# A hybrid retention / HGRN2 / MoE layer: split projections, and the values and gates of all heads ahead of the recurrence

## What is computed

```python
def hg_dir(p, z, lb):
    q = jax.nn.silu(to_heads(p[4], HG_HEADS))
    lbh = lb.reshape(1, HG_HEADS, 1, HG_DK)
    f = lbh + (1.0 - lbh) * jax.nn.sigmoid(to_heads(z, HG_HEADS))
    return q, 1.0 - f, to_heads(p[7], HG_HEADS), jnp.log(f)
...
"""S_t = diag(a_t) S_{t-1} + k_t v_t^T ; o_t = S_t^T q_t, chunkwise."""   # forward and backward, summed
...
b = from_heads(rms_norm(o_hg, hg_norm_w_l)) * jax.nn.silu(p[8])
```

## Time and profile before

| | |
|---|---|
| median of 3 runs | 2821.18 us (2820.17 to 2823.1) |
| profiled execution, its own time | 2818.32 us |
| its span, first to last instruction | 2816.7 us |
| mean granted TensorE clock | 0.978 |
| busy: TensorE, VectorE, ScalarE, GpSimd | 94%, 74%, 51%, 19% |
| `hgrn2` in it | 48.6 to 556.7 us |

### The profile page before, as it was taken

The page is one execution under the profiler, slowest core; times in us unless marked ns, Lnnn a source line. Parts: engine busy times, 40 slices in busy tenths (PEclk is TensorE's granted clock), DMA queues, the critical chain, the costliest instruction groups (busy, mean ns, idle before and its releaser), DMA issues. The chain is left out here.

```text
span 2816.7 us, 43469 instructions
## 1 busy us (share of the span) xinstructions
PE 2651.4 (94%) x15273; PEld 2208.2 (78%) x15274; DVE 2079.2 (74%) x2433; ACT 1426.4 (51%) x1442; POOL 543.3 (19%) x437
## 2 busy tenths in 40 slices
PE   7899999899798899999999999999999999999994
PEld 3668577577687779777887978899989897888783
DVE  4566676673666796999879787866686778967884
ACT  4433535331634574777647565544454546645653
POOL 0524434200013211222121111111121112111110
PEclk9999999999899899999999999999999999999997
DMA  7101100180353796999969787866586769967864
GB/s 260 31 23 31 30 24 16 49 289 1 118 137 124 289 381 218 367 354 351 320 221 363 259 294 262 283 203 205 192 293 207 256 235 329 326 207 272 300 227 134
DMA packets 266663, 596.96 MB, mean 212 GB/s; under 512 B 21373, under 2 KB 47141, under 8 KB 265473
## 3 DMA queue, kind: packets, MB, share of 16 engines
q1 hardware_dynamic: 246208, 552.82, 54.9%
q0 software_dynamic: 20384, 43.19, 6.9%
HBM read 578.01 MB, written 42.25 MB: 220 GB/s over the span
## 5 line engine op out<-in xcount | busy, mean ns | idle before, releaser
L2100 ACT ACTIVATE whi<-e_slot 128x2048 fp32r<-128x2048 f32 x296 | 560.9, 1912 | 437.2 <-PE e_acc L2026 370.8
L2162 DVE TENSOR_TENSOR e_slot_r<-e_slot,whi 128x2048 fp32r<-128x2048 f32 x296 | 674.9, 2287 | 101.1 <-ACT whi L2100 101.1
L2023 PE MATMUL e_acc<-e_xhi,whi 128*128 128x256 f32 x1664 | 399.4, 282 | 3.2 <-ACT e_xhi L2104 3.2
L2100 ACT ACTIVATE whi<-slot 128x2048 fp32r<-128x2048 f32 x148 | 283.3, 1914 | 192.1 <-PE e_acc L1998 192.1
L2162 DVE TENSOR_TENSOR slot_r<-slot,whi 128x2048 fp32r<-128x2048 f32 x151 | 344.7, 2285 | 19.7 <-ACT whi L2100 16.7
L1996 PE MATMUL e_acc<-whi,e_ahi 128*128 128x512 f32 x800 | 319.4, 399 | 0.0
L2023 PEld LDWEIGHTS e_acc<-e_xhi,whi 128*128 128x128 f32 x1664 | 313.1, 188 | 6.3 <-ACT e_xhi L2104 6.3
L1940 POOL DMA_INDIRECT sum<-yo,e_idx_now x50 | 122.3, 2446 | 1012.3 <-issue 539.4
L1998 PE MATMUL e_acc<-whi,e_alo 128*128 128x512 f32 x800 | 313.4, 392 | 0.0
L1997 PE MATMUL e_acc<-e_slot_r,e_ahi 128*128 128x512 f32 x800 | 311.6, 389 | 0.0
L1996 PE MATMUL e_acc<-whi,e_xhi 128*128 128x512 f32 x768 | 303.3, 395 | 0.8 <-DVE e_slot_r L2162 0.5
(11 more groups left out here) (338 smaller groups left out, 4794.8 us busy)
## 6 DMA issues: line engine op xcount, KB each, us to landing
e_slot<-in_w SPq DMA_DIRECT2D x296, 1024.0 KB, 7.1
slot<-in_w SPq DMA_DIRECT2D x151, 1024.0 KB, 7.3
rv<-in_w_ada SPq DMA_DIRECT2D x32, 512.0 KB, 4.7
slot<-in_w_in SPq DMA_DIRECT2D x20, 512.0 KB, 4.1
wa<-in_w_ada SPq DMA_DIRECT2D x8, 1024.0 KB, 17.1
slot<-in_w_in SPq DMA_DIRECT2D x6, 1024.0 KB, 8.6
xt<-in_x SPq DMA_DIRECT2D x8, 512.0 KB, 14.7
slot<-in_w_out SPq DMA_DIRECT2D x4, 1024.0 KB, 13.0
```

The source lines that it names most:

```text
L2023: pe.matmul(out[:, c, :], whi[i % RING][:, w], xhi[:, kk, :], start=first, stop=False, skip_group_check=True)
L2100: act.activation(whi[i % RING][:], raw[i % PIECES][:], ACT.Copy).then_inc(S["whi_made"], 1)
L2162: v.tensor_tensor(wlo[i % PIECES][:], raw[i % PIECES][:], whi[i % RING][:].bitcast(F32), ALU.subtract).then_inc(S["wlo_made"], 1)
```

## The change

All projections of `hgrn2` become split products as in `project_retention`, and the order changes.

- `u` is split once, in `hgrn2`: `high_rows` (ScalarE) and `low_rows` (VectorE), tile by tile, into `uhi` and, over `uT`, `uT_r`. `project_retention` no longer splits `u`, nor its first job's weights, which `high_early` and `low_early` split in head 3.
- Values of all heads come first: ten token tiles x 512 columns (`values`), 24 products a tile, stored to memory (`hg_values`) and loaded again a head at a time.
- Output gates of all heads stand in head 0's start: 16 tiles of 256 columns (`output_gates`), stored (`hg_gates`) and loaded a head at a time. Their sigmoid and product are one instruction each of 1024 columns, the product and the norm weight now on GpSimd.
- Three chunks a head remain, in two places. ScalarE rounds each (`high_chunk`), VectorE takes the remainder (`low_chunk`): two behind the first pick of a head, the third between running sum and last pick but none.
- The six forget-gate groups of head h+1 stand behind the fourth score tile, the first before output 3 and five after it; for heads 1 to 3 the two groups of the last range come last (`z_order`). Keys, sums and queries have one set of buffers, so a copy of a last-range group waits for `lev_ready` of the head before.
- The running sum is done in two halves of 640.

```diff
+            def turned_products(h, i, chunk, a, z):
+                n = group(h, i)
+                if n >= 2:
                     group_read(pe, n - 2)
...
+                pe.wait_ge(S["cw_low"], c + 1)
+                hi, lo = Whi[c % 2], Wlo[c % 2]
+                out = pj[n % 2][:, 0:z - a]
                 for k in range(KT):
+                    pe.matmul(out, hi[:, k, :], uhi[:, k, a:z], start=(k == 0), stop=False)
+                    pe.matmul(out, lo[:, k, :], uhi[:, k, a:z], start=False, stop=False)
+                    mm = pe.matmul(out, hi[:, k, :], ulo[:, k, a:z], start=False, stop=(k == KT - 1))
+                return mm
...
+            values(0, (0, 1))
+            values(1, (0, 1))
+            values(0, (2,))
+            values(1, (2,))
+            for x in range(2, NT):
+                values(x, (0, 1, 2))
+            for i in range(6):
+                gates_of_keys(0, i)
+            queries(0, 0)
+            queries(0, 1)
+            for x in range(6):
+                output_gates(x)
+            turn_keys(0, 0)
+            turn_keys(0, 1)
+            for n in range(2, 6):
+                output_gates(4 + n)
+                turn_keys(0, n)
+            output_gates(10)
+            output_gates(11)
+            updates(0)
+            for x in range(12, 2 * LT):
+                output_gates(x)
...
                 if more:
                     queries(h + 1, 1)
-                    for g in range(3):
-                        values(h + 1, g)
-                        turn_keys(h + 1, 2 * g)
-                        turn_keys(h + 1, 2 * g + 1)
-                    output_gates(h + 1, 0)
+                    for n in range(6):
+                        turn_keys(h + 1, n)
                     updates(h + 1)
-                    output_gates(h + 1, 1)
...
             def copy_z(h, i):
+                if h:
+                    act.wait_ge(S["lev_ready"], 2 * h - (j < 2))
...
+            modulated(0)
+            low_rows(0)
+            low_rows(1)
+            low_values(0)
+            low_values(1)
+            modulated(1)
+            for x in range(2, 6):
+                low_rows(x)
+            modulated(2)
+            for x in range(6, NT):
+                low_rows(x)
```

More of the change, by code:

```diff
@@ L222, in _ @@
                     load_x(i)
-            for n in range(len(keep["h_W"])):
+            for half in range(2):
+                load_value_weights(sp, dram, keep, half)
+            for n in range(2):
                 load_recurrence_weights(sp, dram, keep, n)
@@ L498, in output_gates, with values @@
-            def output_gates(h, g):
-                w = begin(h, 11 + g, 4)
-                for i in range(4):
-                    mm = project(pe, bank(h, 11 + g)[:, i * P:(i + 1) * P], uT, CT + 4 * g + i, w, slice(0, P))
+            def values(x, which):
+                tok = slice(x * P, (x + 1) * P)
+                out = ps[x % 4]
+                if which[0] == 0:
+                    pe.wait_ge(S["u_high"], x + 1)
+                    if x >= 4:
+                        pe.wait_ge(S["v_copied"], x - 3)
+                for n in which:
+                    if n == 1:
+                        pe.wait_ge(S["u_low"], x + 1)
+                    for k in range(KT):
+                        half, c = k // KH, slice(k % KH * 512, (k % KH + 1) * 512)
+                        if x == 0 and n != 1 and k % KH == 0:
+                            pe.wait_ge(S["vw_high" if n == 0 else "vw_low"], half + 1)
+                        mm = pe.matmul(out[:], (uhi, ulo, uhi)[n][:, k, tok], (vhi[half], vhi[half], slots_r[2 + half])[n][:, c], start=(n == 0 and k == 0), stop=(n == 2 and k == KT - 1))
+                if n == 2:
+                    mm.then_inc(S["v_done"], 1)
@@ L705, in roots @@
                 act.activation(ms[:, half * HT:(half + 1) * HT], ms[:, half * HT:(half + 1) * HT], ACT.Sqrt, scale=1.0 / P, bias=eps[:]).then_inc(S["root_ready"], 1)
+            high_values(0)
+            high_rows(0)
+            high_values(1)
+            high_rows(1)
+            for x in range(NT):
+                if x + 2 < NT:
+                    high_rows(x + 2)
+                if x == 3:
+                    high_chunk(0)
+                elif x == 4:
+                    high_chunk(1)
+                elif x == 5:
+                    high_gates(0)
+                value(x)
@@ L707, in _ @@
+            for i in range(6):
+                copy_z(0, i)
+                if i == 4:
+                    high_chunk(2)
             act.wait_ge(S["eps_set"], 1)
             act.wait_ge(S["bounds"], 3)
-            for h in range(-1, HEADS):
-                now, more = h >= 0, h + 1 < HEADS
+            logs(0)
+            query_sig(0, 0)
+            query_sig(0, 1)
+            key_decays(0)
+            output_gate(0)
+            output_gate(1)
+            query_decays(0)
+            output_gate(2)
@@ new lines, in _ @@
+            output_gate(3)
+            high_gates(1)
+            output_gate(4)
+            output_gate(5)
+            turned_keys(0, 0)
+            turned_keys(0, 1)
+            for n in range(2, 6):
+                output_gate(4 + n)
+                turned_keys(0, n)
+                levels(0, 0, (n - 2,))
+            for x in range(10, 2 * LT):
+                output_gate(x)
+                if x < 12:
+                    levels(0, 0, ((4,), (5, 6))[x - 10])
+            high_chunk(3)
@@ L711, in _ @@
+            high_chunk(4)
+            gate_sig(0)
+            for h in range(HEADS):
+                more = h + 1 < HEADS
+                if h and more:
+                    high_chunk(3 * h + 3)
+                    high_chunk(3 * h + 4)
+                if not more:
+                    high_early(0)
+                    high_early(1)
                 if more:
                     copy_z(h + 1, 0)
-                if now:
-                    roots(h, 0)
-                    levels(h, 1, range(0, 2))
+                roots(h, 0)
+                levels(h, 1, range(0, 2))
@@ L735, in _ @@
-                if now:
-                    roots(h, 1)
+                levels(h, 1, range(4, 6))
+                if more:
+                    copy_z(h + 1, 3)
+                levels(h, 1, range(6, NL))
+                if more:
+                    copy_z(h + 1, 4)
+                    copy_z(h + 1, 5)
+                    logs(h + 1)
+                    high_chunk(3 * h + 5)
+                    query_sig(h + 1, 0)
+                else:
+                    for x in range(3):
+                        early_rows(x)
@@ L888, in _ @@
                 if now:
-                    for j in range(HT):
+                    pick(h, 0)
+                    if more:
+                        low_chunk(3 * h + 3)
+                        low_chunk(3 * h + 4)
+                    else:
+                        low_early(0)
+                        low_early(1)
+                    for j in range(1, HT):
                         pick(h, j)
```

534 lines of the change are left out of this document (310 added, 224 removed).

## The result

The changed kernel takes **2866.85 us** (median of 4 runs, 2864.22 to 2867.99). The kernel before takes 2820.68 us in the runs beside it. The ratio is 1.0161, with a 95% interval of 1.0144 to 1.0179: slower by 46 us. The forecast was 2855 in a range of 2834 to 2882. The profiled execution of the changed kernel took 2867.99 us, 49.7 more than the profiled one of before, so some 3 us of what the two traces differ by is only the difference between single executions.

What follows compares the result with a forecast made beforehand. The prediction took a chain on ScalarE, VectorE and GpSimd to bound heads once values and gates leave; start +64.6, shorter heads, longer tail put the stage end at +43.4, less 5.3 gave +38; +34 was taken: 2855, range 2834 to 2882.

Steps and rivals of the forecast that it cites:

- The mechanism: In hgrn2's heads: values and gates cover a chain on other engines; removing 32.2 + 2.8 us of products regains only 9.1.
- The start: Start of hgrn2, where values and output gates move: head 0's scores at 216 against 151.4, +64.6 us.
- The observables: Profile signs: scores near 216, idle some 9 and over 20 us, heads 103 to 107, stage end near 600.
- the clock: TensorE restarts at 1.2 GHz after new waits: 1.6 us before query 0 and 1.7 before each head's scores.
- my own choice: Whole kernel: +38 us with clock losses, +27 without any; +34 was taken.
- the next stage's first product: Start of project_retention: 6.1 us from stage end to first product become about 0.8, -5.3 us.
- the rest: Everything from project_retention's start on: only moves, no stall counted.
- (1) TensorE's work decides: Whole kernel: 73 us less work and 5 at the stage's change, 2743; chance 0.07 for faster, 0.04 for even.
- (2) Less interference of GpSimd and VectorE: Level stretch of heads: levels take 16.6 and 9.0, chain 56, 3 x 5 us less, 2839; chance 0.12.
- (3) The clock stays low through scores: Score tiles take 3.7 instead of 2.0, some 5 us a head, 2880; chance 0.12.
- (4) The run of six groups stalls: Forget gates: last two groups, whose copies wait for level products, hold TensorE; 2860, chance 0.05.
- States beside GpSimd: Gate multiplications moved to GpSimd beside the states: cost taken as 0, bound 3 us a head.

Runs made afterwards that it cites:

- e3: Changed kernel plus additional identity products, result unread, in four TensorE waits, 80 a head in heads 1 to 3; ratio to the kernel before 1.0129.
- e4: Changed kernel with one contraction step of eight in the last eight output-gate tiles; ratio to before 1.0234, total not readable because the router chose other experts.
- e6: Changed kernel with head 0's first four output-gate tiles sent to free PSUM banks; head 0's scores at 204.9, ratio to the kernel before 1.0121.
- e1: Changed kernel with the query chunk's remainder ahead of the second half of the running sum in heads 1 to 3; ratio to the kernel before 1.0122.
- e10: e9 with the level exponentials ahead of the copies of turned keys and fewer additional products; ratio to the kernel before 1.0007.
- e11: e10 without any additional products; ratio to the kernel before 1.0009.
- e5: Changed kernel with e1, e3 and the last output ahead of the query group, all in heads 1 to 3; ratio to the kernel before 1.0082.
- e7: Changed kernel with the edits of e5 and the free banks of e6 together; ratio to the kernel before 1.0045.
- the best of the reordered kernels: e10 with the query chunk's remainder between the two sums, one block size ahead on GpSimd, 32 additional products in updates; ratio to the kernel before 1.0016.
- e8: Changed kernel with one of three products left out in the forget gates of heads 1 to 3; ratio to the kernel before 1.0122.
- e9: e7 with the chain behind the forget gates reordered on VectorE, GpSimd, ScalarE and TensorE; ratio to the kernel before 1.0053.

## Why the prediction was right, point by point

| step | said | measured |
|---|---|---|
| head 0's scores, later by | 64.6 | 65.0 (216.43) |
| idle ahead of the first output gate | 9.4 | 9.12 |
| scores to last forget gate, head 0 | 46 | 46.2 |
| the same, heads 1 and 2 | 43.3 | 44.6, 44.4 |
| last forget gate to next scores | 62.5 | 64.0, 62.7, 63.7 |
| head 3's scores | 536 | 541.85 |
| tail to the next stage's first product | 64.8 | 66.7 |
| that product, later by | 38 | 45.7 |
| rest | 0 | +3.9 in the trace |

- **The mechanism held.** TensorE did less and the kernel took longer, because values and gates had stood in the cover of the chain. e3 shows it from one side (80 products more a head, and no slower), e4 and e6 from the other (less work or less waiting in the start is worth its time nearly in full, up to 12 us).
- **The start** came out within half a microsecond. That timetable was made row by row, bank waits included.
- **The observables**: heads of 110.1, 107.2 and 108.1, said 103 to 107 (by the sum 108.5 for head 0's, 105.8 for the others). TensorE stood idle 20.6 to 21.6 us in each head between second query and scores, most of it ended by states (9.25 and 3.52 above), some by turned keys, none by level products as I had also said; said was over 20. The run of forget gates did not wait for weights. Missed were the stage's end (605.9, said 600) and the next stage's first product (2.65 us on, said within 2).
- **Mis-sized: the clock.** I took 1.6 us for the restart before the query group and 1.7 for that before the scores. The query group took 8.15 instead of the 5.57 of e1, which is 2.6. The restart before the scores cost what I had taken: the fourth score tile starts 12.03 us after the first, and 10.38 in e3, and e10 and e11 differ by 1.7. But in head 1 the clock was low a second time, behind the wait of 1.68 us for a pick (337.81) ahead of the fourth score tile. The ten products of that tile, in the changed kernel, in e3 and in e1:

```profile
339.36 2.44 PE L675 MATMUL h_ps<-h_wq,h_wk 128*128 128x128 f32 x10
```

```profile
335.07 1.38 PE L677 MATMUL h_ps<-h_wq,h_wk 128*128 128x128 f32 x10
```

```profile
332.76 1.38 PE L675 MATMUL h_ps<-h_wq,h_wk 128*128 128x128 f32 x10
```

It cost 1.6 us until the last forget gate, and my sum had no term for it. e1 has the same wait and full clock behind it, which is why its S to Z is shorter; e5 and e7 have the second fall in head 1 (42.9) and not in head 2 (41.3). So 5.8 instead of 3.3 a head: that is where the heads' missing 2 us are.
- **Mis-sized: my own choice.** The sum with clock losses was +38, and I took +34, between it and +27. There was no row for that discount; without it the forecast would have been 2859. Of the 7.7 us between 38 and 45.7, 5.4 are the three heads and 1.9 the tail.
- **Not seen: the next stage's first product** comes 2.65 us after the last one of `hgrn2`, released by a step of TensorE's own queue (608.51 above), where I had 0.8.
- **Not settled: the rest.** I had taken the unchanged rest at 0. It measures 2250.6 to 2262.1 us in these traces for the same code. In the changed kernel 3.0 of the 3.9 us lie in one stretch of `retention`, where the same instructions found another granted clock, before and then after:

```profile
718.46:731.45 12.99, 10.86 (x77) 10.14 (x77) 7.88 (x21) 9.82 (x29) 0.00 (x0) 0.88 0.32 127
```

```profile
763.38:779.42 16.04, 13.92 (x76) 12.99 (x76) 9.27 (x27) 9.82 (x29) 0.00 (x0) 0.70 0.26 104
```

- **The rivals.** (1) TensorE's work decides: refuted by e3. The break-even that I gave for it, 51 us from last forget gate to next scores, was never reached; the best of the reordered kernels has 57.7. (2) Less interference of GpSimd and VectorE: did not come, four of seven blocks ran at half speed in every head, as forecast. (3) The clock stays low through scores: it was between the forecast and this rival, 3.2 instead of 1.7 or 5, and not in one piece. (4) The run of six groups stalls: not in the changed kernel, but e8 shows how near it was: with a third less work the run waits 1.69 us for a copy, and the scores behind it 4.17 for level products.
- **States beside GpSimd**, which I had set at 0 with a bound of 3 us a head: seven steps take 2.65 us both beside GpSimd's gate products (319.31; GpSimd works from 318.55 to 323.3) and without them (323.84). The Trainium skill, GPSIMD Engine Reference, section Specifications, names two SBUF inputs of the VectorE instruction as a condition of their contention; the trace agrees, with 0.41 against 0.83 us for products with two and 2.65 twice for states, one of whose inputs is in PSUM.

## What to carry to other kernels

A busy share of 94% says that an engine always has something to do, not that all of it is on the path: before work is taken out of a stretch, the chain that runs beside it has to be timed, because the cover goes with the work. After that, the waits are the place to look at, since work left out behind a wait buys nothing. Work moved ahead of a pipelined loop is paid there: here nearly in full, and the start could only be shortened by work left out or by a wait that was lifted. And in queues that run in order, look first for the short step that stands behind a long one (here the head's last output behind a query group, a remainder behind a sum, exponentials behind a copy): mending those places, one bank wait and the waits' low clock gave back what the change had cost.

## What was not expected of the hardware

- A running sum over two halves of 640 columns takes 2.87 us alone, and 4.93 beside a difference on GpSimd (e10, 356.15), so that the order of e9 and e10 pays 2 us a head for having both sums beside it. In the changed kernel the second sum at 275.16 takes 2.87.
- GpSimd pays too: the query difference of 1024 columns took 1.92 us (288.41) in the changed kernel, and 3.17 in e10 (372.11), where it began while VectorE multiplied the decayed keys.

```profile
356.15 4.93 DVE L1044 TENSOR_TENSOR_SCAN h_ktok<-h_scan,h_cum 128x640 f32<-128x640 f32 x2
...
372.11 3.17 POOL L972 TENSOR_TENSOR slot<-h_ktok,h_cum 128x1024 f32<-128x1024 f32 x1
```

- The low clock came back within one run of score tiles: 1.65 us for the restart at 326.55 (12.03 instead of 10.38 us from the first tile to the fourth), and 1.6 more behind a wait of only 1.68 us at 337.81. In e1 and e3 the same wait (331.21, 333.52) left the clock high; why is not settled by these runs.
- The same code after the changed stage took 2250.6 to 2262.1 us; why, no run tells (e4, with other experts, left aside). For changes of less than some 10 us in a stage, the stage's own marks and the total have to be read apart.
